# Router products of a hybrid encoder layer: weights stationary on two column halves of the array, tokens moving, the two halves added and turned by one product

## The chip, the cores and the metric

One core of one Trainium2 chip runs the whole kernel. The metric is the device time of one launch in microseconds (us), the median of several runs. The engines are PE (TensorE), DVE (VectorE), ACT (ScalarE), POOL (GpSimd) and SP (SyncE, which issues most DMAs).

## The reference

One layer of a trunk over 1024 tokens of width 1024, all in float32. What is around the change:

```
h = layer_norm(ALPHA*h + hybrid_mixer(h))          # mixer ends in merged @ w_out
scores = sigmoid(h @ w_router)                      # 1024 -> 64 experts
sel = scores + router_bias
# best 4 of 8 groups by the sum of each group's top 2, then top 6 experts
w = scores[top 6] / sum * 2.5
routed = sum of w * expert(h)                       # 64 SwiGLU experts, FF 256
shared = (silu(h @ sg) * (h @ su)) @ sd             # one SwiGLU for all tokens
out = layer_norm(ALPHA*h + routed + shared)
```

## The kernel before, in words

The kernel is written engine by engine: each engine's instructions stand in a fixed order, and semaphores order the engines against each other. After the mixers comes `experts`, whose first part is `norm_and_route` (L2147 on), and in it the change lies. It works on eight tiles of 128 tokens, m = 0 to 7. For each tile:

- PE `mix(m, h)` (L2273): the product with w_out, two halves h of 8 matmuls of 128x512.
- DVE `norm(m)` (L2402 to L2419): sum with the residual, statistics, layer norm; in its middle ACT takes a square root, `std(m)` (L2536).
- PE `turn(m)` (L2283): 8 transposes; ACT `turned(m)` (L2547) copies them to `h1T(m)`, with the model dimension on the partitions.
- PE `logits(m)` (L2297): the router's product, 8 matmuls. The 128 tokens of `h1T` are the stationary operand, the 64 columns of the router's weights `wr` move, and the result is tokens x experts in bank 4. ACT `score(m)` (L2551) is its sigmoid.
- DVE `choose(m)` (L2437 to L2459) finds the six experts, `weigh(m)` (L2464 to L2473) their weights.
- PE `count(m)` (L2308), DVE `placed(m)` (L2479, L2488): each token's place in its expert's list.
- The shared expert, four tiles behind (`DELAY` = 4): PE `up(m)` (L2321, 8 matmuls of 128x512), ACT `gate(m)` (L2557), DVE `hidden(m)` (L2432), PE `turn_hidden(m)` (L2328), ACT `turned_hidden(m)` (L2542), PE `down(m)` (L2337), DVE `sum_base(m)` (L2425).

PE's order in iteration m is: mix(m, 0), turn_hidden(m-5), count(m-3), turn(m-1), mix(m, 1), down(m-5), logits(m-1), up(m-4). DVE's order is: placed(m-3), norm(m), choose(m-1), weigh(m-1), sum_base(m-5), hidden(m-4). So on DVE a tile's hidden activations stand behind the choice of the experts of a later tile, and PE's turn_hidden(m-5) of the next iteration waits for them. ACT's order is: turned_hidden(m-5), turned(m-1), std(m), score(m-1), gate(m-4); root, sigmoid and silu each need a table load ahead. After the loop each engine has a written-out tail, in which the lists of the first experts are made. Two waits of logits(m) matter: for the place counts of an earlier tile (`pos`), and mix(m, 0) waits for the sum of tile m-1 (`sum`):

```
            if m >= 2:
                pe.wait_ge(s["sum"], m)
...
            counted = m if m == NT - 1 else m + 2 - LAG
            if counted > 0:
                pe.wait_ge(s["pos"], counted)
...
        def turn_hidden(m):
            pe.wait_ge(s["hid"], m + 1)
```

Behind this part stand the 65 or more experts' steps (L3150, L3158, L3166, L2762 on PE), which end the kernel.

Of the kernel before, what the change touches and what calls it, by code (L numbers as in the profile page):

```python
# [26 lines left out]
ALU = mybir.AluOpType  # L27
ACT = mybir.ActivationFunctionType
AX = mybir.AxisListType

P = 128
D = 1024
T = 1024
KT = D // P
# [7 lines left out]
NE, TOPK, GROUPS, TOPG = 64, 6, 8, 4  # L42
# [2116 lines left out]
DELAY = 4  # L2159
# [3 lines left out]
def norm_and_route(g, w, joint):  # L2163

    nc, sem, bank = g.nc, g.sem, g.bank
# [3 lines left out]
    wr = g.region(SHARED + 6144, KT, NE)  # L2169
# [3 lines left out]
    def h1T(m):  # L2173
        return merged[:, :, m * P:(m + 1) * P]
# [3 lines left out]
    def take(*dims):  # L2178
        nonlocal at
        ap = g.region(at, *dims)  # L2180
        at += int(np.prod(dims))
        return ap
# [12 lines left out]
    hot, hotg = take(TOPK, NE), take(TOPG, GROUPS)  # L2195
    silu = take(FF)
    before, ones = take(P // 2).bitcast(BF16), take(P // 2).bitcast(BF16)
    assert at <= MERGED

    over, ones64, iota48 = g.over, g.ones64, g.iota48  # L2200
# [8 lines left out]
    g.sums_begun = sem("sums_begun")  # L2209
    s = {n: sem("o_" + n) for n in (  # L2210
        "w wr sum mix st ag ve sd rs xn b T0 Tr lg lgr gu si hid hT hTr dn base iota chain ch cnt pos "
        "made even late clear").split()}
    g.shared_done, g.shared_base = s["dn"], s["base"]
    g.exp_in = [g.keep(f"exp_in{i}") for i in range(4)]
    flat2 = lambda a: bank[:, a:a + 2, :].rearrange("p b n -> p (b n)")
# [2 lines left out]
    def mix_bank(m):  # L2218
        return 6 if m == 1 else 0
# [44 lines left out]
    def tensor(pe, lists):  # L2264
        def mix(m, h, k_range=range(KT)):
            if m >= 2:
                pe.wait_ge(s["sum"], m)
            if h == 0 and m == 0:
                pe.wait_ge(joint.summed, joint.first_half if k_range.start == 0 else joint.units)
            for k in k_range:  # L2270
                if m == 0 and h == 0 and k == WOUT_K:
                    pe.wait_ge(joint.late_in, 16)
                mm = pe.matmul(bank[:, mix_bank(m) + h, :], merged[:, k, m * P:(m + 1) * P], wout[k][:, h * HALF:(h + 1) * HALF],  # L2273
                               start=(k == 0), stop=(k == KT - 1))
            if h == 1 and k == KT - 1:
                mm.then_inc(s["mix"], 1)

        def turn(m):
            pe.wait_ge(s["b"], m + 1)
            if m:  # L2280
                pe.wait_ge(s["Tr"], m)
            for k in range(KT):
                mm = pe.transpose(bank[:, 2 + k // 4, (k % 4) * P:(k % 4 + 1) * P],  # L2283
                                  base[:, m, k * P:(k + 1) * P], g.ident[:])
            mm.then_inc(s["T0"], 1)

        def logits(m):
            pe.wait_ge(s["Tr"], m + 1)
            if m:
                pe.wait_ge(s["lgr"], m)  # L2290
            else:
                pe.wait_ge(s["wr"], 64)
            counted = m if m == NT - 1 else m + 2 - LAG
            if counted > 0:
                pe.wait_ge(s["pos"], counted)
            for k in range(KT):
                mm = pe.matmul(bank[:, 4, 0:NE], h1T(m)[:, k, :], wr[:, k, :], start=(k == 0), stop=(k == KT - 1))  # L2297
            mm.then_inc(s["lg"], 1)

        def count(m):  # L2300
            pe.wait_ge(s["ch"], m + 1)
            pe.wait_ge(s["lgr"], m + 2 if m < NT - 2 else m + 1)
            if m:
                pe.wait_ge(s["pos"], m)
            else:
                pe.wait_ge(s["even"], 1)
            for a in range(m + 1):
                mm = pe.matmul(bank[:, 4, 448:512], before if a == m else ones, chosen[:, a, :],  # L2308
                               start=(a == 0), stop=(a == m))
            if m == NT - 1:  # L2310
                for a in range(NT):
                    mm = pe.matmul(bank[:, 4, 384:448], ones, chosen[:, a, :], start=(a == 0), stop=(a == NT - 1))
            mm.then_inc(s["cnt"], 1)

        def up(m):
            if m:
                pe.wait_ge(s["hid"], m)
            else:
                pe.wait_ge(s["w"], 48)
            for k in range(KT):  # L2320
                mm = pe.matmul(bank[:, up_bank[m], :], h1T(m)[:, k, :], wgu[:, k, :],  # L2321
                               start=(k == 0), stop=(k == KT - 1))
            mm.then_inc(s["gu"], 1)

        def turn_hidden(m):
            pe.wait_ge(s["hid"], m + 1)
            for k in range(2):
                mm = pe.transpose(bank[:, up_bank[m], k * P:(k + 1) * P], hid[:, k * P:(k + 1) * P], g.ident[:])  # L2328
            mm.then_inc(s["hT"], 1)

        def down(m):
            pe.wait_ge(s["hTr"], m + 1)
            if m:
                pe.wait_ge(s["base"], m)
            for h in range(2):
                for k in range(2):
                    mm = pe.matmul(bank[:, 6 + h, :], hidT[:, k, :], wdn[:, k, h * HALF:(h + 1) * HALF],  # L2337
                                   start=(k == 0), stop=(k == 1))
            mm.then_inc(s["dn"], 1)

        joint.tensor(pe)
        pe.wait_ge(g.wout_in, 16)
        for k in (range(0, KT // 2), range(KT // 2, KT)):
            for h in range(2):
                mix(0, h, k)
        for m in range(NT):
            if m:
                mix(m, 0)
            if m > DELAY:
                turn_hidden(m - DELAY - 1)  # L2350
            if m >= LAG:
                count(m - LAG)
            if m:
                turn(m - 1)
                mix(m, 1)
            if m < NT - 1:
                if m > DELAY:
                    down(m - DELAY - 1)
                if m:
                    logits(m - 1)  # L2360
                if m >= DELAY:
                    up(m - DELAY)
        logits(6)
        up(3)
        count(5)
        turn(7)
        down(2)
        count(6)
        turn_hidden(3)
        logits(7)  # L2370
        up(4)
        count(7)
        down(3)
        turn_hidden(4)
        up(5)
        lists(0)
        down(4)
        turn_hidden(5)
        up(6)
        lists(1)  # L2380
        down(5)
        turn_hidden(6)
        up(7)
        lists(2)
        down(6)
        turn_hidden(7)
        first.last_down = lambda: down(NT - 1)
# [145 lines left out]
    def scalar(act):  # L2533
        def std(m):
            act.wait_ge(s["ve"], m + 1)
            act.activation(rstd[:], rstd[:], ACT.Sqrt).then_inc(s["sd"], 1)  # L2536

        def turned_hidden(m):
            act.wait_ge(s["hT"], m + 1)
            if m:  # L2540
                act.wait_ge(s["dn"], m)
            act.activation(hidT.rearrange("p k n -> p (k n)"), bank[:, up_bank[m], 0:FF],  # L2542
                           ACT.Copy).then_inc(s["hTr"], 1)

        def turned(m):
            act.wait_ge(s["T0"], m + 1)
            act.activation(h1T(m), flat2(2).rearrange("p (k n) -> p k n", k=KT), ACT.Copy).then_inc(s["Tr"], 1)  # L2547

        def score(m):
            act.wait_ge(s["lg"], m + 1)  # L2550
            act.activation(scores[:, m, :], bank[:, 4, 0:NE], ACT.Sigmoid).then_inc(s["lgr"], 1)  # L2551

        def gate(m):
            act.wait_ge(s["gu"], m + 1)
            if m:
                act.wait_ge(s["hid"], m)
            act.activation(silu, bank[:, up_bank[m], 0:FF], ACT.Silu).then_inc(s["si"], 1)  # L2557

        joint.scalar(act)
        for m in range(NT):  # L2560
            if m > DELAY:
                turned_hidden(m - DELAY - 1)
            if m:
                turned(m - 1)
            std(m)
            if m:
                score(m - 1)
            if m >= DELAY:
                gate(m - DELAY)
        turned(7)  # L2570
        turned_hidden(3)
        score(7)
        gate(4)
        turned_hidden(4)
        gate(5)
        turned_hidden(5)
        gate(6)
        turned_hidden(6)
        gate(7)
        turned_hidden(7)  # L2580

    def gpsimd(pool, gather):
# [10 lines left out]
        counted(g.iota[:], [[1, P]], 0, 0).then_inc(s["made"], 1)  # L2593
        counted(g.pad_row[:], [[0, 1]], T + 1, 1).then_inc(s["made"], 1)
        pool.memset(ones, 1.0).then_inc(s["made"], 1)
        pool.memset(before, 1.0).then_inc(s["made"], 1)
        pool.wait_ge(s["made"], 5)
        pool.affine_select(out=before, in_=before, compare_op=ALU.is_gt, fill=0.0, base=0,
# [11 lines left out]

    first = Shared()
    first.sync, first.tensor, first.vector, first.scalar, first.gpsimd = sync, tensor, vector, scalar, gpsimd
    return first

# [703 lines left out]
```

## Time and profile before

| | |
|---|---|
| median of 3 runs | 2087.28 us (2085.93 to 2087.61) |
| the profiled execution | 2086.21 us |
| its span | 2084.5 us |
| PE busy | 2002.2 us (96%) |
| DVE busy | 1137.3 us (55%) |
| POOL busy | 772.4 us (37%) |
| ACT busy | 504.6 us (24%) |
| mean granted clock of TensorE | 0.987 |

The profile is of one execution. Its span is from the first to the last instruction; its time holds 1.7 us more. A matmul of float32 operands stands in the profile as two passes, so 8 matmuls are x16. Successive passes overlap, since a pass's latency is longer than the distance to the next: the time that a group takes from PE is the distance between its start and the start of the group behind it, not its busy time. A rate of 1.00 in the column PEclk is 2.4 GHz, 0.50 is 1.2 GHz.

### The profile page before, as it was taken

The numbers are of one execution on the slowest core, as the hardware profiler recorded it, in microseconds if no ns is written. First come the engines' busy times: TensorE is split into PE (matmuls) and PEld (weight loads), VectorE is DVE, ScalarE is ACT, GpSimd is POOL, SyncE is SP. The second block draws the span as 40 slices with busy tenths as digits, with TensorE's granted clock in tenths as the row PEclk, the third lists the DMA queues.
The fourth block names the chain that finished last, engine by engine and source line by source line (L and its number), as shares of the span: only waits on it lengthen the run. The fifth ranks groups of instructions, "written<-read, shape, count | busy, mean of one in ns | idle before, by whom it ended". The sixth has DMA issues, their size and how long they took to land.

```text
span 2084.5 us, 23703 instructions
## 1 busy us (share of the span) xinstructions
PE 2002.2 (96%) x7237; PEld 1017.2 (49%) x7238; DVE 1137.3 (55%) x3065; ACT 504.6 (24%) x1102; POOL 772.4 (37%) x717
## 2 busy tenths in 40 slices
PE   7999999999999999999989999999999999999992
PEld 6444667575544444544435554444444444444440
DVE  6221546776611223335666656866666666666645
ACT  3111554452321223214432220011111111111113
POOL 1752005612122222115880002455454454455441
PEclk9999999999999999999999999999999999999996
DMA  5421000011142122243253106899999999999974
GB/s 146 135 82 41 21 21 22 21 46 46 49 144 72 65 71 81 68 148 123 84 208 147 41 31 237 309 337 354 349 351 357 357 357 358 349 353 355 350 253 170
DMA packets 129640, 370.45 MB, mean 178 GB/s; under 512 B 33713, under 2 KB 65669, under 8 KB 103833
## 3 DMA queue, kind: packets, MB, share of 16 engines
q1 hardware_dynamic: 103960, 314.83, 40.2%
q0 software_dynamic: 23520, 54.61, 10.8%
q8 instruction: 44, 0.72, 0.1%
q10 hardware_dynamic: 2080, 0.01, 0.1%
q14 instruction: 36, 0.29, 0.0%
HBM read 320.57 MB, written 68.17 MB: 186 GB/s over the span
## 4 chain that ended last, share of the span: by engine, by line
PE 47%; DVE 3%; DMA 2%; issue 1%; POOL 1%; ACT 0%; SPq 0%; DVEq 0%; POOLq 0%
PE banks L3150 20%; PE banks L3166 10%; PE banks L2273 5%; PE banks L2007 5%; PE banks L2321 2%; DMA arena<-in_w_exp_down_dram 2%; PE banks L279 1%; POOL arena L2129 1%; PE banks L2337 1%; PE banks L2762 1%; PE banks L3158 1%; PE banks L2297 1%; DVE arena L3143 0%; DVE arena L3226 0%; DVE index L3113 0%
## 5 line engine op out<-in xcount | busy, mean ns | idle before, releaser
L3150 PE MATMUL banks<-arena 128*128 128x512 f32 x1056 | 470.5, 598 | 6.2 <-DVE arena L3143 3.5
L3129 POOL DMA_INDIRECT arena<-h_rows,index x268 | 278.7, 1040 | 154.4 <-DVE index L3113 75.4
L3150 PEld LDWEIGHTS banks<-arena 128*128 128x128 f32 x1056 | 195.8, 190 | 230.4 <-issue 226.4
L1719 PE MATMUL banks<-arena 128*128 128x512 f32 x672 | 299.0, 594 | 1.1 <-ACT arena L323 1.1
L3166 PE MATMUL banks<-arena 128*128 128x512 f32 x528 | 237.6, 593 | 1.3 <-ACT arena L2965 0.8
L3143 DVE STREAM_TRANSPOSE arena<-arena 128x1024 f32<-128x1024 f32 x66 | 133.9, 2029 | 136.4 <-PE banks L3150 136.4
L3137 POOL DMA_INDIRECT sums<-arena,row_to x66 | 107.8, 1633 | 269.4 <-DMA sums<-arena,row_to 241.2
L279 PE MATMUL banks<-arena 128*128 128x512 f32 x416 | 193.5, 602 | 2.5 <-PEq L108 2.2
L1719 PEld LDWEIGHTS banks<-arena 128*128 128x128 f32 x672 | 123.1, 190 | 135.7 <-issue 134.0
L3113 DVE TENSOR_SCALAR index<-row 32x1 uint32<-32x1 f32 x1072 | 155.4, 145 | 17.1
L3166 PEld LDWEIGHTS banks<-arena 128*128 128x128 f32 x528 | 100.2, 190 | 127.0 <-issue 125.3
L776 PE MATMUL banks<-arena 128*128 128x512 f32 x336 | 145.1, 593 | 2.7 <-ACT arena L604 2.5
L285 PE MATMUL banks<-arena 128*128 128x256 f32 (+1 forms) x640 | 143.8, 366 | 0.0
L2960 ACT ACTIVATE arena<-banks 128x256 f32<-128x256 f32 x65 | 24.9, 383 | 434.8 <-PE banks L3150 434.8
L2007 PE MATMUL banks<-arena 128*128 128x512 f32 x280 | 123.8, 603 | 5.4 <-issue 4.7
L2273 PE MATMUL banks<-arena 128*128 128x512 f32 x256 | 114.1, 600 | 2.5 <-POOL arena L2129 2.5
L285 PEld LDWEIGHTS banks<-arena 128*128 128x128 f32 x640 | 105.4, 190 | 19.2 <-issue 10.1
L279 PEld LDWEIGHTS banks<-arena 128*128 128x128 f32 x416 | 74.9, 192 | 75.7 <-issue 73.9
L776 PEld LDWEIGHTS banks<-arena 128*128 128x128 f32 x336 | 63.4, 190 | 83.0 <-issue 78.0
L2972 ACT ACTIVATE arena<-banks,weight 128x512 f32<-128x512 f32 x64 | 44.0, 687 | 203.6 <-PE banks L3166 203.6
L2007 PEld LDWEIGHTS banks<-arena 128*128 128x128 f32 x280 | 53.8, 193 | 75.2 <-issue 73.2
L2873 DVE TENSOR_SCALAR arena<-banks,weight 128x512 f32<-128x512 f32 x64 | 48.0, 750 | 75.6 <-PE banks L3166 75.6
(400 smaller groups left out, 2427.9 us busy)
## 6 DMA issues: line engine op xcount, KB each, us to landing
arena<-in_w_exp_gate_dram SPq DMA_DIRECT2D x66, 1024.0 KB, 8.7
arena<-in_w_exp_up_dram SPq DMA_DIRECT2D x66, 1024.0 KB, 11.2
arena<-in_w_exp_down_dram SPq DMA_DIRECT2D x66, 1024.0 KB, 19.1
arena<-in_w_in_dram SPq DMA_DIRECT2D x26, 1024.0 KB, 5.3
gates<-arena SPq DMA_DIRECT2D x60, 256.0 KB, 2.0
arena<-gates SPq DMA_DIRECT2D x15, 1024.0 KB, 7.8
arena<-h_rows,index POOLq DMA_INDIRECT x268, 8.0
arena<-in_x_dram SPq DMA_DIRECT2D x8, 512.0 KB, 5.9
```

The costliest lines, as they stand in the source:

```text
L279: mm = pe.matmul(bank[0:width], w[:, q, col:col + width], g.hT[:, q, at * HALF:(at + 1) * HALF], start=(q == 0), stop=(q == KT - 1))
L285: mm = pe.matmul(bank[:, m * width:(m + 1) * width], g.hT[:, k, (at + m) * P:(at + m + 1) * P], w[:, k, col:col + width], start=(k == 0), ...
L776: mm = pe.matmul(block_bank(n, b), left[:, k, :], right[:, k, :], start=(alone and k == 0), stop=(k == 3), skip_group_check=True)
L1719: mm = pe.matmul(gate_bank(n, b), left[:, k, :], right[:, k, :], start=(alone and k == 0), stop=(k == 3), skip_group_check=True)
L2007: mm = pe.matmul(product_bank(n, c), lhs[:, k, :], rhs[:, k, :], start=(alone and k == 0), stop=(k == deep[b] - 1), skip_group_check=True)
L2273: mm = pe.matmul(bank[:, mix_bank(m) + h, :], merged[:, k, m * P:(m + 1) * P], wout[k][:, h * HALF:(h + 1) * HALF], start=(k == 0), stop=( ...
L3113: ins = dve.tensor_scalar(g.index[32 * b:32 * b + 32, k, q:q + 1], g.row[32 * q:32 * q + 32, k, :], 4.0, float(b), ALU.mult, ALU.add)
L3129: return pool.indirect_dma_start(w.x[k][:, 256 * q:256 * (q + 1)], None, rows, bass.IndirectOffsetOnAxis(ap=g.index[:, k, q:q + 1], axis=0 ...
L3137: return pool.indirect_dma_start(g.sums, bass.IndirectOffsetOnAxis(ap=g.row_to[:, b:b + 1], axis=0), w.y[k], None, bounds_check=last, oob_ ...
L3143: return dve.transpose(w.xT.rearrange("p k (q n) -> p q k n", q=4), w.x[k].rearrange("p (q n k) -> p q k n", q=4, k=KT))
L3150: mm = pe.matmul(g.bank[:, 2, :].rearrange("p (a f) -> p a f", a=2), xT[:, k, :], wgu[:, :, k, :], start=(k == 0), stop=(k == KT - 1))
L3166: mm = pe.matmul(g.bank[:, 4 + h, :], hidT[:, k, :], wdn[:, k, h * HALF:(h + 1) * HALF], start=(k == 0), stop=(k == 1))
```

## The change

`logits(m)` exchanges the operands. For each of four steps it issues two matmuls, c = 0 and 1, whose stationary operand is a 64-column piece of `wr` and whose moving operand is the 128 tokens of `h1T`; c = 0 adds up the first four pieces of the model dimension in partitions 0 to 63 of the bank, c = 1 the last four in partitions 64 to 127. ACT copies the 128x128 result (`partial`, before `std` in its order) to `logit_parts`. A further matmul `logit_sum`, with `logit_parts` stationary and `both` (two identity matrices of 64, one above the other) moving, adds the halves and turns them, so that the scores are tokens x experts as before. POOL makes `both` once. PE's order has logit_sum(0) to (2) inside the next mix, after its second matmul, and logit_sum(3) to (6) behind the next up. In the tail down(2), logits(7) and turn_hidden(3) change places.

```
-            for k in range(KT):
-                mm = pe.matmul(bank[:, 4, 0:NE], h1T(m)[:, k, :], wr[:, k, :], start=(k == 0), stop=(k == KT - 1))
-            mm.then_inc(s["lg"], 1)
+            for k in range(KT // 2):
+                for c in range(2):
+                    mm = pe.matmul(bank[c * NE:(c + 1) * NE, 4, P:2 * P], wr[:, 4 * c + k, :], h1T(m)[:, 4 * c + k, :],
+                                   start=(k == 0), stop=(k == KT // 2 - 1), skip_group_check=True)
+            mm.then_inc(s["lp"], 1)
+
+        def logit_sum(m):
+            pe.wait_ge(s["lpr"], m + 1)
+            if m == 0:
+                pe.wait_ge(s["both"], 1)
+            pe.matmul(bank[:, 4, 0:NE], logit_parts, both, start=True, stop=True,
+                      skip_group_check=True).then_inc(s["lg"], 1)
...
             for k in k_range:
+                if h == 0 and k == 2 and 2 <= m <= DELAY:
+                    logit_sum(m - 2)
...
                 if m >= DELAY:
                     up(m - DELAY)
+                    logit_sum(m - 1)
         logits(6)
         up(3)
+        logit_sum(6)
+        down(2)
         count(5)
         turn(7)
-        down(2)
         count(6)
+        logits(7)
         turn_hidden(3)
-        logits(7)
+        logit_sum(7)
         up(4)
...
+        def partial(m):
+            act.wait_ge(s["lp"], m + 1)
+            act.activation(logit_parts, bank[:, 4, P:2 * P], ACT.Copy).then_inc(s["lpr"], 1)
...
             if m:
                 turned(m - 1)
+                partial(m - 1)
             std(m)
             if m:
                 score(m - 1)
...
         turned(7)
+        partial(7)
         turned_hidden(3)
         score(7)
...
+        pool.tensor_tensor(both, g.ident[:, 0:NE], g.ident[:, NE:P], ALU.add).then_inc(s["both"], 1)
```

Place 1: PE from mix(5, 1) to turn_hidden(1), before (L2273 mix, L2337 down, L2297 logits, L2321 up, L2328 turn_hidden, L2308 count):

```order
L2273 MATMUL banks<-arena 128x512 x8
L2337 MATMUL banks<-arena 128x512 x4
L2297 MATMUL banks<-arena 128x64 x8
L2321 MATMUL banks<-arena 128x512 x8
L2273 MATMUL banks<-arena 128x512 x8
L2328 MATMUL banks<-ident,arena 128x128 x2
L2308 MATMUL banks<-arena 128x64 x4
```

The same stretch now (L2276 mix, L2349 down, L2301 logits, L2333 up, L2309 logit_sum, L2340 turn_hidden, L2320 count):

```order
L2276 MATMUL banks<-arena 128x512 x8
L2349 MATMUL banks<-arena 128x512 x4
L2301 MATMUL banks<-arena 64x128 x8
L2333 MATMUL banks<-arena 128x512 x8
L2309 MATMUL banks<-arena 128x64
L2276 MATMUL banks<-arena 128x512 x8
L2340 MATMUL banks<-ident,arena 128x128 x2
L2320 MATMUL banks<-arena 128x64 x4
```

The product that ends the logits stands behind the eight matmuls of up; between it and turn_hidden stands only one half of mix.

Place 2: PE's tail from logits(6) to up(4), before (L2283 turn):

```order
L2297 MATMUL banks<-arena 128x64 x8
L2321 MATMUL banks<-arena 128x512 x8
L2308 MATMUL banks<-arena 128x64 x6
L2283 MATMUL banks<-ident,arena 128x128 x8
L2337 MATMUL banks<-arena 128x512 x4
L2308 MATMUL banks<-arena 128x64 x7
L2328 MATMUL banks<-ident,arena 128x128 x2
L2297 MATMUL banks<-arena 128x64 x8
L2321 MATMUL banks<-arena 128x512 x8
```

and now (L2286 turn):

```order
L2301 MATMUL banks<-arena 64x128 x8
L2333 MATMUL banks<-arena 128x512 x8
L2309 MATMUL banks<-arena 128x64
L2349 MATMUL banks<-arena 128x512 x4
L2320 MATMUL banks<-arena 128x64 x6
L2286 MATMUL banks<-ident,arena 128x128 x8
L2320 MATMUL banks<-arena 128x64 x7
L2301 MATMUL banks<-arena 64x128 x8
L2340 MATMUL banks<-ident,arena 128x128 x2
L2309 MATMUL banks<-arena 128x64
L2333 MATMUL banks<-arena 128x512 x8
```

logit_sum(6) stands behind up(3); down(2) has moved ahead of count(5), so that between the turn and count(6) nothing is left.

Place 3: ACT in an iteration from m = 5 on, now (L2557 turned_hidden, L2562 turned, L2566 partial, L2551 std, L2570 score, L2576 gate):

```order
L2557 ACTIVATE arena<-banks 128x256
L2562 ACTIVATE arena<-banks 128x8x128
L2566 ACTIVATE arena<-banks 128x128
L2551 ACT_TABLE_LOAD
L2551 ACTIVATE rstd<-rstd 128x1
L2570 ACT_TABLE_LOAD
L2570 ACTIVATE arena<-banks 128x64
L2576 ACT_TABLE_LOAD
L2576 ACTIVATE arena<-banks 128x256
```

The copy L2566 is new, and it stands ahead of the root and of the root's table load.

## Rows read from the trace of the kernel before

**Rows 1.** The page: busy time of PE

```profile
PE 2002.2 (96%) x7237; PEld 1017.2 (49%) x7238; DVE 1137.3 (55%) x3065; ACT 504.6 (24%) x1102; POOL 772.4 (37%) x717
```

**Rows 2.** PE's waits from 1060 to 1330 us, then from 1330 us to the end

```profile
PE banks L2297 <- DVE arena L2488: 1.8, 1, 1.8
...
PE banks L2762 <- issue: 2.0, 1, 2.0
```

**Rows 3.** Timeline of PE, logits(4) to turn_hidden(1): start, busy us, what

```profile
1183.62 1.90 PE L2297 MATMUL banks<-arena 128*128 128x64 f32 x16
1185.35 7.09 PE L2321 MATMUL banks<-arena 128*128 128x512 f32 x16
1192.27 7.03 PE L2273 MATMUL banks<-arena 128*128 128x512 f32 x16
1199.14 0.38 PE L2328 MATMUL banks<-ident,arena 128*128 128x128 f32 x2
```

**Rows 4.** Timeline of PE and DVE around logits(0)

```profile
1100.37 7.03 PE L2273 MATMUL banks<-arena 128*128 128x512 f32 x16
1107.24 1.89 PE L2297 MATMUL banks<-arena 128*128 128x64 f32 x16
1107.44 1.22 DVE L2402 SCALAR_TENSOR_TENSOR arena<-arena,banks 128x1024 f32<-128x1024 f32 x1 [8.41 <-PE banks L2273]
1108.97 7.08 PE L2273 MATMUL banks<-arena 128*128 128x512 f32 x16
```

**Rows 5.** Timeline of PE in a mixer that uses column halves at 128 moving columns

```profile
750.65 7.03 PE L1719 MATMUL banks<-arena 128*128 128x512 f32 x16
757.62 1.31 PE L1772 MATMUL banks<-arena 128*64 128x128 f32 x20
758.86 1.35 PE L1744 MATMUL banks<-arena 64*128 64x512 f32 x8
...
912.19 1.73 PEld L1772 LDWEIGHTS banks<-arena 128*64 128x64 f32 x32 [0.76 <-issue]
```

**Rows 6.** Timeline of ACT and DVE: a 128x128 copy, then score(4) to norm(6)

```profile
914.21 0.28 ACT L1881 ACTIVATE arena<-banks 128x128 f32<-128x128 f32 x1 [1.31 <-PE banks L1772]
...
1185.55 0.22 ACT L2551 ACTIVATE arena<-banks 128x64 f32<-128x64 f32 x1 [0.59 <-PE banks L2297]
1186.41 0.22 DVE L2437 TENSOR_TENSOR arena<-arena 128x64 f32<-128x64 f32 x1
1194.31 1.22 DVE L2425 SCALAR_TENSOR_TENSOR arena<-arena,banks 128x1024 f32<-128x1024 f32 x1
1195.45 0.41 DVE L2432 TENSOR_TENSOR arena<-arena,banks 128x256 f32<-128x256 f32 x1
1201.62 1.28 ACT L2536 ACT_TABLE_LOAD   x1
1207.51 1.22 DVE L2402 SCALAR_TENSOR_TENSOR arena<-arena,banks 128x1024 f32<-128x1024 f32 x1 [7.38 <-PE banks L2273]
```

**Rows 7.** Timeline of PE and DVE in the tail, logits(6) to up(4)

```profile
1234.34 1.89 PE L2297 MATMUL banks<-arena 128*128 128x64 f32 x16
1240.56 0.22 DVE L2437 TENSOR_TENSOR arena<-arena 128x64 f32<-128x64 f32 x1
1249.54 0.20 DVE L2488 TENSOR_SCALAR arena<-arena 128x64 f32<-128x64 f32 x1
1249.88 2.61 PE L2297 MATMUL banks<-arena 128*128 128x64 f32 x16 [1.75 <-DVE arena L2488]
1252.28 8.16 PE L2321 MATMUL banks<-arena 128*128 128x512 f32 x16
```

**Rows 8.** Clock after waits: a window's busy times (PE first) and PEclk, then timeline rows

```profile
1252.00:1254.00 2.00, 2.00 (x5) 1.07 (x5) 1.11 (x11) 1.45 (x2) 0.00 (x0) 0.50 1.00 309
...
1301.43 8.83 PE L3150 MATMUL banks<-arena 128*128 128x512 f32 x16 [2.69 <-DVE arena L3143]
...
105.93 93.00 PE L776 MATMUL banks<-arena 128*128 128x512 f32 x216 [2.49 <-ACT arena L604]
```

More of the change, by code:

```diff
@@ L2197, in norm_and_route @@
     before, ones = take(P // 2).bitcast(BF16), take(P // 2).bitcast(BF16)
+    logit_parts, both = take(P), take(NE)
     assert at <= MERGED
@@ L2211, in norm_and_route @@
         "w wr sum mix st ag ve sd rs xn b T0 Tr lg lgr gu si hid hT hTr dn base iota chain ch cnt pos "
-        "made even late clear").split()}
+        "made even late clear lp lpr both").split()}
     g.shared_done, g.shared_base = s["dn"], s["base"]
```

## The prediction

> **What bounds the kernel.** The page first: PE is busy 96% of the span [rows 1]. The chain of waits and the list of who waited for whom say where the rest is. From 1060 to 1330 us, the part with the router, one wait is at a router product, 1.8 us [rows 2]; from 1330 us to the end its longest wait is 2.0 us. So behind this part the kernel is one long queue on PE, and what this part gains or loses comes out at the end in full. The timeline of PE then gives prices as distances between starts. Half of mix takes 1107.24 - 1100.37 = 6.87 us, a router product 1108.97 - 1107.24 = 1.73 [rows 4], up 1192.27 - 1185.35 = 6.92 [rows 3], of which I count 0.05 as the router product's way out, since the mix behind one also takes 6.92. So a router product costs PE 1.78 us now.
>
> What the reader should look for is not only that price but the slack behind it. score(4) runs at 1185.55, choose(4) starts on DVE at 1186.41, and hidden(1) ends at 1195.45 + 0.41 = 1195.86 [rows 6]. PE asks for it at 1199.14 [rows 3]. The slack is 3.3 us.
>
> **The products themselves.** The column halves are in the trace already: 20 passes with 64 stationary and 128 moving columns stand between 757.62 and 758.86 [rows 5], and 32 loads of this form fit in 1.73 us, so a pass costs 0.054 us and 16 cost 0.86. The way in is 757.62 - 750.65 - 6.87 = 0.10, the way out 1.24 - 20 x 0.054 = 0.16, together 1.13 (rounded up by 0.01). That is 0.65 less than 1.78, eight times. A 64-column pass of today costs 1.73 / 16 = 0.108 [rows 4]; logit_sum has two of the same form, 0.22, and I count 0.25 with its entry. Net -0.40 a tile, -3.2 us if nothing else changed.
>
> The halves share all rows of the array, and the Trainium skill ("TensorE: Matmul & The Clock Gate", Part 3, The mechanism) says that a weight load runs beside matmuls in flight only when their row groups differ. By that rule the halves would not overlap at all. The passes at 0.054 us, half of the 0.108 above, speak against it; it is a rival below. "TensorEngine Tiling (Array Packing)", Key Properties, in the same skill says that a change of tiling mode drains the array. The trace agrees that switching costs something, the 0.10 and 0.16 above.
>
> **Tiles 0 to 2 on PE.** mix(m, 0) waits for DVE's sum of tile m-1, which starts 0.20 after the mix and takes 1.22 [rows 4]; with the semaphore's way that is 1.48. The router product of 1.78 hid it; one of 1.13 leaves PE 0.35 idle. Cost now 1.13 + 0.35 + 0.25 = 1.73 against 1.78: -0.05 each, -0.15 for three. The copy on ACT is done long before the sum is issued, 1.72 us into the mix: 0.20 + 0.28 [rows 6] after the product.
>
> **The new wait, iterations 5 to 7.** logit_sum(m-1) now stands behind up, and before hidden(m-4) DVE must do choose and weigh, which need its score. From the issue of logit_sum(4): 0.20 to ACT (the usual distance, as 1107.24 to 1107.44 in [rows 4]), sigmoid 0.22, 0.04 to DVE, then choose to hidden 1195.86 - 1186.41 = 9.45 [rows 6], 0.07 back to PE: 9.98. PE has between the two only one half of mix, 6.87. So turn_hidden(1) waits 3.11 us, and turn_hidden(2) the same. For turn_hidden(0) there is no sum_base in DVE's order, 1.20 less (distance from L2425 to L2432 in [rows 6] and its rounding): 1.91. Together 8.13 us. Each shift passes to all that follows, so the next stall is not smaller. The saving on PE at the products of tiles 3 to 5, which begin these stretches, is 3 x 0.40 = 1.20.
>
> What is queued behind the waiting turn_hidden is count, turn and the other half of mix; all of PE stands. On ACT the new copy stands ahead of the root (with its 1.28 table load [rows 6]). Where down comes before the router product, the root comes about 3 us late (1.13 + 0.20 + 0.28 + 1.28). The score is later still, and DVE is idle 7.38 us before its next sum [rows 6]. That delay costs nothing; without this cover it would cost 3 us a tile. The table load for silu now comes between score and gate, but hidden is behind 7.9 us of choosing, so it is hidden too. The instruction on POOL runs once beside idle time; DMA issues move with the tiles.
>
> **The tail.** From logits(6) to up(4) PE took 1252.28 - 1234.34 = 17.94 [rows 7]; 2.61 - 1.89 = 0.7 of it is clock, so 17.3 at full speed. Now: product 1.13, up 6.87, logit_sum 0.25, to ACT and DVE 0.46, then DVE from choose(6) to the place counts of tile 6, 1249.74 - 1240.56 = 9.18 [rows 7], 0.06 back: 17.95, when logits(7) may start. Then 1.13, the copy and its ways 0.52, logit_sum 0.25: 19.85. That is +2.56. count(7) then waits 0.07 for the choice, since score(7) stands behind turned_hidden(3) and a table load.
>
> Sum at full clock: -0.15 - 1.20 + 8.13 + 2.56 + 0.07 = **+9.4 us**.
>
> **The clock.** After the 1.75 us wait the granted clock was 0.50 in a 2 us window, that is 1.2 GHz [rows 8], and the two groups took 0.72 and 1.07 longer than their like, 1.8 us [rows 7]. After a 2.69 us wait a group took 8.83 against 7.03, again 1.8; after one of 2.49 us none was lost, for 216 passes at 0.43 are 93 us [rows 8]. What went before differed each time. The tail loses its 1.8 before and after alike. The new waits of 3.11 us should mostly cost 1.8 each; at 1.91 it is even. I take two of three: +3.6, with 0 and 5.4 as the ends. The skill's first page named above (Part 1) says that an idle stretch throttles the array to half clock; the trace agrees with that in two of these three waits.
>
> Sum +13.0, on the profiled execution's 2086.2 (span 2084.5 and 1.7 around it) 2099.2; the median shown is 1.1 higher, so I say **2100.3**. With 5.4 it is 2102.1, without any clock loss 2096.7.
>
> **The rivals.**
> 1. The waits come, but the clock holds (the 2.49 us row for, two others against): +9.4, 2096.7. Chance 0.18.
> 2. The halves do not overlap, by the rule above: 16 passes at 0.108 make 1.73 + 0.26 = 1.99 for 1.13, 0.86 more for each of 8 tiles, less 3 x 0.35 that was idle: +5.8 more, 2106 with clock. 0.04.
> 3. Faster. DVE's chain fits: this decides if logit_sum to turn_hidden is under 6.87 instead of 9.98, which asks for choose and weigh to shrink from 7.9 to 4.8 us. Then the 3.2 us are saved, and with the tail's wait of 1.75 and its clock loss of 1.8 gone, -6.7: 2080.5. Against it: the 1194.31 - 1186.41 = 7.9 us of choosing [rows 6] are the same instructions after as before. 0.03.
> 4. The waits are real but small, or a gain of only 3.2 us: within 0.2% (4 us, about what a measurement of this kernel can tell from no change). 2084 to 2091. 0.05.
>
> The forecast, with one to three clock losses, gets the remaining 0.70. Ranges: its own is 2097.5 to 2103. To hold eight in ten I go down past rival 1 to 2094, and up to 2104.5 for somewhat longer ways in and out. Slower 0.92 (forecast, rivals 1 and 2), same 0.05, faster 0.03.
>
> **What would show it.** In the profile after: router products of x16 passes 128*64 with the next group 1.1 us behind them; PE idle at turn_hidden (L2340) three times, 1.9, 3.1 and 3.1 us, released by DVE's hidden; a wait of about 2 us at count(6) and 2.9 at logits(7) for DVE's place counts; idle of 0.35 at three mixes; a PEclk below 0.8 behind the 3.1 us waits; the first expert's up some 13 us later. It is wrong if turn_hidden does not wait, or if the first expert starts earlier than at 1301.4.

## The result, and the profile after

| | before | after |
|---|---|---|
| median | 2087.45 us (4 runs, 2085.93 to 2089.03) | 2101.67 us (4 runs, 2098.08 to 2102.62) |
| ratio, 95% interval | | 1.0065 (1.005 to 1.008) |
| profiled execution | 2086.21 us, span 2084.5 | 2098.08 us, span 2096.3 |
| PE busy | 2002.2 us | 2001.7 us |

The changed kernel is 14 us slower by the medians and 11.9 us slower between the two profiled executions (11.8 by their spans). The page after shows that PE does slightly less and stands more:

```profile
PE 2001.7 (95%) x7253; PEld 1011.9 (48%) x7254; DVE 1137.0 (54%) x3065; ACT 507.2 (24%) x1110; POOL 774.9 (37%) x718
```

PE's waits from 1060 to 1345 us in the changed kernel: engine and line that waited, who released it, us in total, times, the longest.

```profile
PE banks L2340 <- DVE arena L2447: 7.5, 3, 2.9
PE banks L2301 <- DVE arena L2503: 2.8, 1, 2.8
...
PE banks L2320 <- DVE arena L2503: 1.9, 1, 1.9
...
PE banks L2276 <- DVE arena L2417: 1.0, 3, 0.4
```

The first line is new: three times turn_hidden (L2340) waits for DVE's hidden (L2447). The second and third answer to [rows 2], where the place counts cost one wait of 1.8 us. The fourth is the sum that the mixes of tiles 2 to 4 wait for.

The timeline of one iteration of the changed kernel, PE rows first, then the ACT and DVE rows that lead to the wait; it answers to [rows 3] and [rows 6]:

```profile
1185.86 1.09 PE L2301 MATMUL banks<-arena 128*64 128x128 f32 x16
1186.88 7.13 PE L2333 MATMUL banks<-arena 128*128 128x512 f32 x16
1193.86 0.33 PE L2309 MATMUL banks<-arena 128*128 128x64 f32 x2
1194.02 7.09 PE L2276 MATMUL banks<-arena 128*128 128x512 f32 x16
1203.99 0.69 PE L2340 MATMUL banks<-ident,arena 128*128 128x128 f32 x2 [2.88 <-DVE arena L2447]
```

```profile
1187.00 0.28 ACT L2566 ACTIVATE arena<-banks 128x128 f32<-128x128 f32 x1 [10.31 <-PE banks L2301]
1188.59 0.20 ACT L2551 ACTIVATE rstd<-rstd 128x1 f32<-128x1 f32 x1
1194.22 0.22 ACT L2570 ACTIVATE arena<-banks 128x64 f32<-128x64 f32 x1 [4.13 <-PE banks L2309]
1194.48 0.23 DVE L2452 TENSOR_TENSOR arena<-arena 128x64 f32<-128x64 f32 x1 [2.85 <-ACT arena L2570]
1202.39 1.22 DVE L2440 SCALAR_TENSOR_TENSOR arena<-arena,banks 128x1024 f32<-128x1024 f32 x1
1203.53 0.41 DVE L2447 TENSOR_TENSOR arena<-arena,banks 128x256 f32<-128x256 f32 x1
```

The router product costs PE 1186.88 - 1185.86 = 1.02 us to the next group, which is what was wanted. Its sum waits out all of up, so that the score runs at 1194.22, choose starts at 1194.48, and hidden ends at 1203.53 + 0.41 = 1203.94. PE has issued the half of mix by 1194.02 + 6.87 = 1200.89 and then stands for 3.10 us (the profile counts 2.88, from the end of the last pass on).

### The profile page after: what moved, and what is told of

The parts are those of the page before. It is cut to its first block, busy times and chain, and to the rows that moved or that the text cites. A ratio compares the mean times of both kernels' runs of the same rounds, so it can differ in the third digit from the quotient of the medians.

```text
span 2096.3 us, 23745 instructions
## 1 busy us (share of the span) xinstructions
PE 2001.7 (95%) x7253; PEld 1011.9 (48%) x7254; DVE 1137.0 (54%) x3065; ACT 507.2 (24%) x1110; POOL 774.9 (37%) x718
## 4 chain that ended last, share of the span: by engine, by line
PE 46%; DVE 4%; DMA 2%; issue 2%; POOL 1%; ACT 0%; SPq 0%; POOLq 0%; DVEq 0%
PE banks L3172 20%; PE banks L3188 10%; PE banks L2007 5%; PE banks L2276 4%; PE banks L2333 3%; PE banks L279 1%; DMA sums<-arena,row_to 1%; POOL arena L2129 1%; DMA arena<-in_w_exp_down_dram 1%; PE banks L2349 1%; PE banks L2784 1%; PE banks L3180 1%; DVE arena L3248 0%; DVE index L3135 0%; DVE arena L3165 0%
## 5 line engine op out<-in xcount | busy, mean ns | idle before, releaser
L2276 PE MATMUL banks<-arena 128*128 128x512 f32 x256 | 115.3, 602 | 3.5 <-POOL arena L2129 2.5
```

## The experiments

Each short diff is against the changed kernel unless said otherwise. The kernel before was timed beside the first four (2087.24 us, 25 runs) and beside the last three (2086.5 us, 22 runs). Its single runs lay between 2083.1 and 2093.9, so differences of less than about 2 us rest on the profiles.

The profiled executions can't be compared by their absolute times. In the nine of them the part with the router starts anywhere from 1082.99 to 1087.02 us, and from the first expert's up to the end they take 782.2 to 786.3 us. So the table counts from the 32 passes of mix that open the part to the first expert's up. These opening passes run at a lowered clock in all nine, for nearly the same time (15.45 to 15.70 us), so the last column leaves them out. The two ends in the kernel before (the second end is in [rows 8]) and in the changed one:

```profile
1084.19 15.47 PE L2273 MATMUL banks<-arena 128*128 128x512 f32 x32 [2.54 <-POOL arena L2129]
```

```profile
1084.53 15.47 PE L2276 MATMUL banks<-arena 128*128 128x512 f32 x32 [2.53 <-POOL arena L2129]
...
1312.68 8.83 PE L3172 MATMUL banks<-arena 128*128 128x512 f32 x16 [2.69 <-DVE arena L3165]
```

| kernel | the part, us | against before | waits in it behind which PE ran slowly |
|---|---|---|---|
| before | 217.24 | | logits(7) |
| changed | 228.15 | +10.9 | turn_hidden(1), logits(7) |
| e1 | 220.50 | +3.3 | logits(7) |
| e2 | 221.06 | +3.8 | logits(7) |
| e3 | 229.68 | +12.4 | logits(7) |
| e4 | 215.13 | -2.1 | none |
| e5 | 213.91 | -3.3 | none |
| e6 | 214.75 | -2.5 | none |
| e7 | 226.90 | +9.7 | turn_hidden(2), logits(7) |

### e1: the sums inside up

```
         def up(m, inner=None):
...
             for k in range(KT):
+                if inner is not None and k == 2:
+                    logit_sum(inner)
...
-                    up(m - DELAY)
-                    logit_sum(m - 1)
+                    up(m - DELAY, m - 1)
```

> The changed kernel with one thing moved: logit_sum(3) to (5) stand inside up, after its second matmul, instead of behind its eighth; the tail stays. Theory A (the place of logit_sum behind up makes turn_hidden wait for DVE's hidden): the three waits of 1.8, 2.9 and 2.9 us at turn_hidden fall to 0.5 or less each, about 7 us, and the clock losses behind them go with them (1.8 us each where they fell); the first expert's up starts about 2 us later than before the change, and the time is 2089 to 2091. Rival B (hidden is late for another reason, the root behind the new copy on ACT): the waits stay at 2 us or more and the time stays above 2096.

Measured: 2090.18 us, 1.0012 of the kernel before (1.0002 to 1.0022). The three waits at turn_hidden have gone from the list of waits; the same iteration in the timeline now reads:

```profile
1186.81 1.09 PE L2301 MATMUL banks<-arena 128*64 128x128 f32 x16
1187.84 1.98 PE L2335 MATMUL banks<-arena 128*128 128x512 f32 x4
1189.66 0.33 PE L2309 MATMUL banks<-arena 128*128 128x64 f32 x2
1189.83 5.37 PE L2335 MATMUL banks<-arena 128*128 128x512 f32 x12
1195.03 7.03 PE L2276 MATMUL banks<-arena 128*128 128x512 f32 x16
1202.01 0.44 PE L2342 MATMUL banks<-ident,arena 128*128 128x128 f32 x2
```

turn_hidden (L2342) starts 6.98 us behind the mix, 0.11 more than the mix takes. Theory A holds. ACT's order, which rival B blamed, is unchanged here. By the medians 11.5 of the 14.2 us went with the place of three matmuls. In the traces it is 7.7 of 10.9: the 8.2 us of standing and a slow stretch of 1.5 behind one of the waits are gone, and the slow stretch behind logits(7) is 1.2 us longer in this execution (11.23 us from logits(7) to count(7), where the changed kernel takes 10.06). The rest of the 11.5 is not located. The first expert was expected 2 us later than before the change; counted as in the table it is 3.3.

### e2: hidden ahead of choose on DVE

```
             norm(m)
+            if m >= DELAY:
+                hidden(m - DELAY)
             if m:
                 choose(m - 1)
                 if m == NT - 1:
-                    hidden(m - DELAY)
                     placed(m - 2)
...
-            if DELAY <= m < NT - 1:
-                hidden(m - DELAY)
```

> The changed kernel with only DVE's order changed: hidden(m-4) stands ahead of choose(m-1) instead of behind weigh and sum_base; PE's and ACT's orders stay. Theory A (PE waits for hidden because 7.9 us of choosing stand in front of it, once the score is late): no wait at turn_hidden; the choice of tile 6 is as late as before, so the tail keeps its waits, the one at count(6) grows by up to 1.7 us; in all 2090 to 2092. Rival (PE waits for the choice itself, through count): the waits move from turn_hidden to count and the time stays at 2098 to 2102.

Measured: 2091.81 us, 1.0021 (1.001 to 1.0032). The sums are as late as in the changed kernel, but PE no longer waits at turn_hidden. Its list of waits from 1060 to 1345 us begins with:

```profile
PE banks L2320 <- DVE arena L2503: 3.6, 1, 3.6
PE banks L2301 <- DVE arena L2503: 2.8, 1, 2.8
```

The wait at count(6) (L2320) grew from 1.9 to 3.6, as worked out. So it is the order of DVE that turned a late score into a standing PE at turn_hidden. In the loop the choice itself could be late for nothing, hidden behind it could not; in the tail the late choice still costs PE the two waits above.

### e3: one half after the other

```
-            for k in range(KT // 2):
-                for c in range(2):
+            for c in range(2):
+                for k in range(KT // 2):
```

> The changed kernel with the two loops of the router product exchanged: all four matmuls of the first column half, then all four of the second. Theory A (two column halves run side by side only where their passes alternate): a product takes some 16 x 0.108 = 1.7 us plus 0.26 of switching instead of 1.02 to the next group; 0.9 more in 5 of 8 tiles and 0.5 more in the three that waited for the sum anyway, together +5 to +6 us on the changed kernel, 2103 to 2108. Rival B (a pass of this form costs 0.054 us by itself, whatever stands beside it, because its 64-column weight load is half as long): no difference, 2098 to 2103, and 1.02 us again.

Measured: 2100.14 us, 1.006 (1.0043 to 1.0076), in total not to be told from the changed kernel. That is inside rival B's range and below theory A's; the profile decides. First the changed kernel, then e3, both at tile 0: the product and the group behind it.

```profile
1107.67 1.09 PE L2301 MATMUL banks<-arena 128*64 128x128 f32 x16
1109.05 1.98 PE L2276 MATMUL banks<-arena 128*128 128x512 f32 x4 [0.29 <-DVE arena L2417]
```

```profile
1109.27 1.58 PE L2301 MATMUL banks<-arena 128*64 128x128 f32 x16
1110.78 1.98 PE L2276 MATMUL banks<-arena 128*128 128x512 f32 x4
```

The product takes 1110.78 - 1109.27 = 1.51 us instead of 1.02. Rival B, for which the product should not change, falls. Theory A said some 1.9 and is right in kind, too large in size. Three windows within e3's product show why. The columns are busy us of PE and of its weight loads, each with the number of passes in that window, then PEclk.

```profile
1109.20:1109.70 0.50, 0.43 (x4) 0.43 (x5) 1.00 1.01 401
1109.70:1110.10 0.40, 0.40 (x10) 0.40 (x8) 1.00 1.10 440
1110.10:1110.80 0.70, 0.70 (x10) 0.51 (x6) 1.00 1.00 398
```

In the changed kernel the first 0.43 us of the product hold twice as many:

```profile
1107.60:1108.10 0.50, 0.43 (x8) 0.43 (x10) 1.00 1.04 418
```

A pass lasts 0.27 us and counts in every window that it touches. In e3's first window 4 passes start in 0.43 us, one about every 0.11 us: one half alone. The second window holds 10 in 0.40 us, where one half alone could show some 6 ((0.40 + 0.27) / 0.11), so passes of both halves run there. That the second half starts as soon as its first pass is near enough in the order is a reading of these counts, not shown by itself. Alternating makes the halves run side by side from the start. The 0.49 us that e3 loses per product are hidden in three of eight tiles by the 0.35 us wait for the sum, so some 2.9 us (5 x 0.49 + 3 x 0.14) should remain. The medians don't resolve that, but the table does: e3's part is 1.5 us longer than the changed kernel's, though it has no slow stretch at turn_hidden and the changed kernel has one of 1.5; together 3.0.

### e4: all sums inside, the tail in the old order

As e1, and in PE's tail:

```
         logits(6)
-        up(3)
-        logit_sum(6)
-        down(2)
+        up(3, 6)
         count(5)
         turn(7)
+        down(2)
         count(6)
-        logits(7)
         turn_hidden(3)
-        logit_sum(7)
-        up(4)
+        logits(7)
+        up(4, 7)
```

> As e1, and the tail in the order of the kernel before, with logit_sum(6) inside up(3) and logit_sum(7) inside up(4). Theory A: the waits at count(6) go, logits(7) waits 2.1 to 2.4 us for the place counts of tile 6 (before the change 1.75), the first expert's up starts within 0.7 us of where it did before, and the time is 2086 to 2088: what the products save is spent on sums and waits. Rival: with all sums out of the way the full saving of 3.2 us comes out, 2084.

Measured: 2086.19 us, 0.9995 (0.9985 to 1.0004): no difference from the kernel before. PE's waits:

```profile
PE banks L2301 <- DVE arena L2502: 2.1, 1, 2.1
...
PE banks L2276 <- DVE arena L2416: 1.0, 3, 0.4
PE banks L2320 <- DVE arena L2473: 0.3, 1, 0.3
```

With the exchange in place and nothing late, the gain is close to nothing: what the products give, the products that add the halves, the longer wait at logits(7) (2.1 for 1.8), the new one at count(7) (0.3) and the three waits of 0.35 for DVE's sum take back in good part. The rival's 2084 lies below the interval's lower end (0.9985 x 2087.24 = 2084.1) by a hair, so the time alone hardly refutes it. The table does: the part is 2.1 us shorter than before, but the kernel before ran slowly behind its wait at logits(7), 1.8 us of loss [rows 7], and e4 did not, behind a longer wait. That leaves some 0.3 us for the exchange, not 3.2. The expected place of the first expert, within 0.7 us of the old one, is missed by the same clock loss.

### e5: and the place counts ahead of weigh

```
-                weigh(m - 1)
                 if m == NT - 1:
                     placed(m - 1)
+                weigh(m - 1)
```

on top of e4.

> As e4_sums_inside, and in DVE's tail placed(6) stands ahead of weigh(6), so that the place counts of tile 6 are there 2.7 us earlier. Theory A (what is left of the wait at logits(7) is weigh(6) in front of placed(6)): the wait falls from 2.1 to about 0.5 us and the clock loss behind it goes; a wait of up to 0.8 at count(7) comes. The first expert's up starts at about 1297.5 and the time is 3 us under the kernel before, 2083 to 2085. Rival: the time won is lost again at count(7), since weigh(6) now delays choose(7); then the time is that of e4_sums_inside.

Measured: 2084.0 us, 0.9989 (0.998 to 0.9998).

```profile
1246.78 1.09 PE L2301 MATMUL banks<-arena 128*64 128x128 f32 x16 [0.46 <-DVE arena L2502]
...
1255.74 0.41 PE L2320 MATMUL banks<-arena 128*128 128x64 bf16 x8 [0.58 <-DVE arena L2473]
...
1296.90 9.80 PE L3171 MATMUL banks<-arena 128*128 128x512 f32 x16 [2.69 <-DVE arena L3164]
```

logits(7) waits 0.46 us, its 16 passes run at full clock (1.09), and count(7) now waits 0.58. Its part is 3.3 us shorter than before the change, and 1.2 us shorter than e4's; neither e4 nor e5 has a slow stretch in it.

### e6: the kernel before, with only that

The same edit of DVE's tail in the kernel before the change.

> The kernel before the change with only that: placed(6) ahead of weigh(6). Theory A: the wait at logits(7) falls from 1.75 to 0.5 us and the clock loss of 1.8 us behind it goes, a wait of 0.4 at count(7) comes; 2.5 to 3 us faster than the kernel before, 2084.5. The exchange of the operands is then worth 1.0 us or less (e5 against this). Rival: the exchange carries the gain, then this kernel stays at 2087 and e5 alone is faster.

Measured: 2084.81 us, 0.9984 (0.9974 to 0.9994).

```profile
1247.94 1.97 PE L2297 MATMUL banks<-arena 128*128 128x64 f32 x16 [0.47 <-DVE arena L2488]
1249.74 7.09 PE L2321 MATMUL banks<-arena 128*128 128x512 f32 x16
```

The wait is 0.47 and the slow stretch behind it is gone: 1.97 and 7.09 us for the 2.61 and 8.16 of [rows 7]. The expected wait of 0.4 at count(7) is not in the list. This kernel and e5 are both faster than the kernel before by about 0.1%, and their intervals lie over each other, so the times can't tell them apart. Most of the gain comes from the order of two steps on DVE, and the rival, by which e6 gains nothing, is refuted. The traces settle what is left: neither execution has a slow stretch in the part, and e5's is 214.75 - 213.91 = 0.84 us shorter. That is what the exchange is worth where nothing waits for it (the medians differ by 0.81), one trace of each.

### e7: the kernel before, its product behind up

Against the kernel before:

```
-                if m:
-                    logits(m - 1)
                 if m >= DELAY:
                     up(m - DELAY)
+                if m:
+                    logits(m - 1)
```

> The kernel before the change with its old product, but logits(3) to (5) issued behind up instead of in front of it, so that the score is as late as in the changed kernel. Theory A (lateness alone costs): waits of 1.9, 3.1 and 3.1 us (measured in the changed kernel: 1.8, 2.9, 2.9) at turn_hidden, plus 1.8 us of clock behind two or three of them; nothing changes in the tail; 2098 to 2101. Rival B (the new form, its copy on ACT or its switches of tiling cause the waits): the waits stay under 1 us and the time is 2087 to 2089.

Measured: 2098.39 us, 1.0052 (1.0034 to 1.007). The old form, with no copy, no sum and no switch of tiling, shows the same wait:

```profile
PE banks L2328 <- DVE arena L2432: 7.5, 3, 2.9
```

7.5 us in three, as in the changed kernel, to the tenth. Rival B falls: the lateness alone is enough. Of the two or three clock losses expected here the trace has one, of 1.5 us.

## Why the prediction was right

The time (2101.67 for 2100.3, range 2094 to 2104.5), the sign and the main term came out. The sum at full clock is right, +9.4 forecast and 10.9 - 1.5 = 9.4 in the trace (a slow stretch behind logits(7) is there before and after); two smaller terms, tiles 0 to 2 and the tail, missed by 0.3 and 0.6 us in opposite directions. That the median is met too is partly luck, as told under the clock. Step by step, from the profiled execution after, in distances between starts:

- **The products.** Forecast 1.13 us with the ways in and out. Measured 1.02, and 0.10 in front (1107.67 - 1100.70 - 6.87), so 1.12. That passes of two halves run at 0.054 us each could be read off another stage of the same kernel [rows 5].
- **logit_sum.** Forecast 0.25. To the next group it takes 1194.02 - 1193.86 = 0.16, but up in front of it now takes 1193.86 - 1186.88 = 6.98, where up takes 6.87 behind down (e7, 1185.58 to 1192.45). Product and sum together save what was forecast, 0.40 a tile: from down to the next mix 1192.27 - 1180.18 = 12.09 us before ([rows 3] has the second) and 1194.02 - 1182.33 = 11.69 after. With 1.12 for the product that leaves 1.78 - 0.40 - 1.12 = 0.26 for the sum.

```profile
1180.18 3.60 PE L2337 MATMUL banks<-arena 128*128 128x512 f32 x8
```

```profile
1182.33 3.60 PE L2349 MATMUL banks<-arena 128*128 128x512 f32 x8
```

- **Tiles 0 to 2.** Forecast a wait of 0.35 at each mix; measured 0.29, 0.35 and 0.35. The step as a whole was slightly wrong: -0.15 was forecast for the three tiles, and they take 0.19 more than before. A mix with the sum inside takes 1116.25 - 1109.05 = 7.20 us, 0.33 more than 6.87.
- **turn_hidden.** Forecast 1.91, 3.11 and 3.11 us. Measured by starts 1174.19 - 1165.35 - 6.87 = 1.97, then 3.10 and 3.10. Forecast sum 8.13, measured 8.17. That it came out to the tenth is no luck: the chain is built from the same DVE instructions before and after. e1 and e2 remove it in two independent ways, e7 makes it without the rest of the change.
- **The root behind the new copy.** Forecast 3 us late at no cost. It ran at 1188.59; DVE waited 3.25 us for it where it waited 0.27 before, and was still idle 2.85 us in front of choose. The cover held.
- **The tail.** Forecast 19.85 for 17.3 us at full clock. logits(7) started 1261.47 - 1243.54 = 17.93 us behind logits(6), for the forecast 17.95. The 1.90 from there to up(4) were 2.74, at the low clock; what they are at full clock no run shows. To up(4) the tail grew by 20.67 - 17.94 = 2.7, but the two hold different parts of their clock losses. To count(7), behind which both run at full clock again, it grew from 1260.28 - 1234.34 = 25.94 to 1271.53 - 1243.54 = 27.99: +2.05, where 2.63 (2.56 + 0.07) was forecast. The waits at count(6) and logits(7) were forecast as 2 and 2.9, and were 1.87 and 2.80.
- **The clock.** This is the step that was off. Forecast two losses of 1.8 us among the three waits, 3.6 in all. The profiled execution has one, behind the second wait:

```profile
1204.00:1206.00 2.00, 2.00 (x12) 1.94 (x13) 0.42 (x2) 0.39 (x1) 0.00 (x0) 0.50 0.65 262
...
1238.00:1240.00 2.00, 2.00 (x6) 0.82 (x5) 0.00 (x0) 0.00 (x0) 0.00 (x0) 1.00 0.00 0
```

At 1204 the clock was at 0.50 (1.2 GHz), behind a wait of 2.88; at 1238, behind one of 2.89, it was at 1.00. The slow turn and its neighbours took 1213.59 - 1203.99 = 9.60 us, where the same groups took 8.14 behind the first wait (1174.19 to 1182.33): 1.5 us lost, not 1.8. With one loss the sum is 9.4 + 1.5 = 10.9, and the first expert indeed started 1312.68 - 1301.43 = 11.3 us later, of which 0.3 came from before this part (1084.53 against 1084.19). The same waits stand in e3 and e7: e3 has no loss behind any of the three, e7 one behind the third. So of nine such waits in three traces two were followed by a loss, both by 1.5 us, and the three short ones never; "mostly 1.8 each" was too much.

The forecast of the median hit because two misses cancel. The clock term was 2.1 us too large for the profiled execution, and the median lies 2101.67 - 2098.08 = 3.6 us above that execution, not 1.1 as in the kernel before. The other three runs are 3.5 to 4.5 us longer than the profiled one, with mean clocks of 0.982 to 0.984 for 0.986. Clock losses at the other two waits would fit that, but so would losses outside the part: the nine traces differ by 4 us ahead of it and by 4 us behind it. These three runs left no trace, so the cause of the 3.6 us stays open.

Rival 1 (no clock loss) is refuted by the window above for the profiled execution; e3's execution, with the same waits, is what it describes. Rival 2 (the halves don't overlap) is refuted by the 1.02 us, and e3 shows what less overlap looks like. Rival 3 asked for a chain of under 6.87 us; it was 9.97 (1194.02 to 1203.99). Rival 4's small wait was not there; it came true only in e4, which takes the waits out.

The Trainium skill ("TensorE: Matmul & The Clock Gate", Part 3, The mechanism) has weight loads overlap with running matmuls only where row groups differ. The two column halves share all rows, and their products still ran side by side, 1.02 us for 16 passes; in the window of 0.50 us above, loads and passes are both busy for the same 0.43 us. For this form the measurement decides against the rule. That the halves would then not overlap at all was a step of the prediction, since the rule is about loads.

## What to carry to other kernels

Before a product is split into a part and a later sum, walk from the new place of its result along each engine that reads it, and look at what stands behind the reader in that engine's order: here 0.4 us saved per tile (product and sum together) made up to 3.1 us of waiting, because an unrelated step (hidden) was queued behind the choice that needed the sum. A slack of 3.3 us can be read off the profile in one subtraction, and a move of 7 us does not fit into it. And look at the one wait that is already there: in the traces, swapping two steps of DVE in front of it took 2.5 us off the part (1.8 of them the clock loss behind the wait, which not every execution has), the faster product 0.3 to 0.8.

## What the runs showed of the hardware that was not expected

- Which waits of PE are followed by a lower clock is not settled by their length: of two waits of 2.88 and 2.89 us in the changed kernel the first lost 1.5 us and the second nothing; in e7 it was the other way round, 2.88 at 1204 without a loss, 2.89 at 1234 with one; in e3 neither lost anything. Two rows of e7:

```profile
1204.54 1.07 PE L2283 MATMUL banks<-ident,arena 128*128 128x128 f32 x8
...
1235.09 1.95 PE L2283 MATMUL banks<-ident,arena 128*128 128x128 f32 x8
```

Both groups are eight transposes close behind such a wait, 1.07 us and 1.95 us.

- Nor is it settled by which instructions stand before the wait. The one of 2.49 us in [rows 8] stands in all nine kernels behind the same ones. Five traces have no loss behind it (93.0 us for the 216 passes), four have one of 1.6 to 1.7 us (in them the granted clock from 100 to 120 us is 0.91 on average), as e1:

```profile
106.97 94.66 PE L776 MATMUL banks<-arena 128*128 128x512 f32 x216 [2.51 <-ACT arena L604]
```

These four reach the group 0.2 to 1.1 us later than the other five. So by what these traces show a clock loss can be forecast only as a chance, and a single execution is one draw. Lengths do not order it either: e4 lost nothing behind 2.11 us at logits(7), the kernel before lost 1.8 behind 1.75.

- Issue order decides how much of two column halves overlaps: alternating 1.02 us for 16 passes, one half after the other 1.51.
